# Scores of two neighbouring attention maps, issued together in different rows of the TensorE array

## The reference, cut to what matters

```python
h = rmsnorm(x, ln1_g[layer])
qa, ka, va, cq, ckv, kr, qc, kc, vc = split(h @ w_in[layer])
out_a = mixer_dilated(...)   # A: 6 heads of width 64, local bands (128,1) (512,4) (2048,16)
out_b = mixer_mla(...)       # B: 6 heads, q and k of width 64 + 32 = 96
out_c = mixer_diff(...)      # C: 4 heads with 2 softmax maps each, q and k of width 32
x = x + concat([out_a, out_b, out_c]) @ w_o[layer]
u = rmsnorm(x, ln2_g[layer]) @ w_up[layer]
x = x + square(relu(u)) @ w_down[layer]
```

## Time and profile before

| | |
|---|---|
| median of 3 runs | 1770.53 us (1770.4 to 1772.18) |
| the profiled execution | 1770.33 us, its span 1768.6 us |
| granted TensorE clock, mean | 0.999 |
| PE busy | 1757.6 us, 99% |
| PEld (weight loads) busy | 1535.5 us, 87% |
| DVE busy | 1157.6 us, 65% |
| ACT busy | 931.6 us, 53% |
| POOL busy | 26.5 us, 1% |
| DMA | 303 MB, mean 171 GB/s |

### The profile page before, as it was taken

How to read it: one execution, slowest core, us unless ns; L and a number is a source line. 1 busy time by engine, 2 the same in 40 slices (tenths; PEclk the granted TensorE clock), 3 DMA queues, 4 the chain that set the end, 5 groups by cost and what they waited for, 6 DMA issues and landing times.

```text
span 1768.6 us, 26182 instructions
## 1 busy us (share of the span) xinstructions
PE 1757.6 (99%) x9886; PEld 1535.5 (87%) x9886; DVE 1157.6 (65%) x1700; ACT 931.6 (53%) x1376; POOL 26.5 (1%) x32
## 2 busy tenths in 40 slices
PE   9999999999999999999999999999999999999998
PEld 8888898898888988898889888889898888989886
DVE  6665588766655666468776664668574746857473
ACT  6554456645544555455655553567553536745352
POOL 0000000000000000000000000000000000000000
PEclk9999999999999999999999999999999999999999
DMA  8755533544555554543345545544355543435551
GB/s 315 214 190 179 203 117 122 190 175 182 186 180 189 191 190 179 202 167 120 134 176 175 190 178 190 185 133 146 116 193 198 184 163 118 145 115 194 197 185 48
DMA packets 45842, 303.04 MB, mean 171 GB/s; under 512 B 5104, under 2 KB 6256, under 8 KB 12312
## 3 DMA queue, kind: packets, MB, share of 16 engines
q1 hardware_dynamic: 45720, 301.36, 48.5%
HBM read 300.02 MB, written 1.31 MB: 170 GB/s over the span
## 4 chain that ended last, share of the span: by engine, by line
PE 97%; DVE 1%; ACT 1%; issue 1%; POOLq 0%; POOL 0%; ACTq 0%; DVEq 0%
PE psG L493 13%; PE psG L495 13%; PE psG L494 13%; PE psG L571 9%; PE psP L571 5%; PE psSO L571 5%; PE psG L577 5%; PE psG L544 3%; PE psG L545 3%; PE psG L546 3%; PE psSO L577 3%; PE psP L577 3%; PE psSO L688 2%; PE psP L610 1%; PE psP L870 1%; PE psSO L894 1%
## 5 line engine op out<-in xcount | busy, mean ns | idle before, releaser
L1596 DVE TENSOR_TENSOR wlo<-raw,whi 128x1024 fp32r<-128x1024 f32 (+4 forms) x388 | 656.6, 1705 | 311.0 <-ACT whi L1074 310.7
L1074 ACT ACTIVATE whi<-raw 128x1024 fp32r<-128x1024 f32 (+4 forms) x388 | 554.0, 1443 | 276.0 <-PE psG L495 162.2
L493 PE MATMUL psG<-whi,x 128*128 128x512 f32 (+3 forms) x544 | 210.8, 387 | 0.0
L495 PE MATMUL psG<-whi,x 128*128 128x512 f32 (+3 forms) x544 | 200.8, 369 | 0.0
L494 PE MATMUL psG<-wlo,x 128*128 128x512 f32 (+3 forms) x544 | 200.4, 368 | 0.0
L493 PE MATMUL psG<-whi,hid_hi 128*128 128x512 f32 x472 | 184.1, 390 | 0.0
L495 PE MATMUL psG<-whi,hid_lo 128*128 128x512 f32 x472 | 183.6, 389 | 0.0
L494 PE MATMUL psG<-wlo,hid_hi 128*128 128x512 f32 x472 | 183.6, 389 | 0.0
L571 PE MATMUL psG<-x,whi 128*128 128x512 f32 x704 | 179.8, 392 | 0.0
L544 PE MATMUL psG<-x,wlo 128*128 128x256 f32 x512 | 147.5, 288 | 1.5 <-DVE wlo L1596 1.5
L571 PEld LDWEIGHTS psG<-x,whi 128*128 128x128 f32 x704 | 126.6, 189 | 22.6
(11 more groups left out here) (380 smaller groups left out, 2778.7 us busy)
## 6 DMA issues: line engine op xcount, KB each, us to landing
raw<-in_w SPq DMA_DIRECT2D x261, 1024.0 KB, 4.8
raw<-in_w SPq DMA_DIRECT2D x12, 768.0 KB, 4.2
raw<-in_w SPq DMA_DIRECT2D x14, 512.0 KB, 3.3
raw<-in_w SPq DMA_DIRECT2D x4, 576.0 KB, 3.8
raw<-in_w SPq DMA_DIRECT2D x4, 432.0 KB, 3.2
bias<-line_scratch SPq DMA_DIRECT2D x8, 192.0 KB, 10.1
h<-in_x SPq DMA_DIRECT2D x2, 512.0 KB, 5.6
out<-h SPq DMA_DIRECT2D x2, 512.0 KB, 2.7
```

The source lines that it names most:

```text
L493: e.matmul(o, ph, wh, start=first, stop=False)
L495: i = e.matmul(o, pl, wh, start=False, stop=last)
L1074: e.activation(w_at(whi, j, off, n), raw[:, j % RAW, off:off + n], ACT.Copy).then_inc(s_hi, count)
L1596: e.tensor_tensor(w_at(wlo, j, off, n), raw[:, j % RAW, off:off + n], f32(w_at(whi, j, off, n)), ALU.subtract).then_inc(s_lo, count)
```

## The change

Maps whose scores use 32 or 64 rows (C and A: n below 8 or from 14) are issued in pairs. At the even map's step PE takes two banks, for n and n + 1, and issues the matmuls in the order: first query block of n, first of n + 1, second of n, second of n + 1. The odd map's step issues no scores. The order of everything else on PE within a step stays. B stays as it was. On DVE each map's scores are still read in that map's own step, but the wait is for the scores of the pair's second map in both cases.

```diff
+def paired(n):
+
+    return n < 8 or n >= 14
@@ tensor
             def scores2(l, n):
-                q, kk, _, _, _ = map2(n)
+
+                if paired(n) and n % 2:
+                    return
                 e.wait_ge(s_prep, prep_value(l, "qc", 0) if n < 8 else prep_value(l, "qb", 2) if n < 14 else prep_value(l, "ka", 1))
-                b = spare(("s2", l, n))
+                ns = (n, n + 1) if paired(n) else (n,)
+                bs = [spare(("s2", l, m)) for m in ns]
                 for t, c0, w in SEGS:
-                    i = e.matmul(TB[b][:, c0:c0 + w], q[:, t * 128:t * 128 + 128], kk[:, 0:w], start=True, stop=True)
-                i.then_inc(s_tp, 1)
-                spare_frees(b, (s_mx, 2 * (16 + 20 * l + n) + 2))
+                    for m, b in zip(ns, bs):
+                        q, kk, _, _, _ = map2(m)
+                        i = e.matmul(TB[b][:, c0:c0 + w], q[:, t * 128:t * 128 + 128], kk[:, 0:w], start=True, stop=True)
+                        if t == 1:
+                            i.then_inc(s_tp, 1)
+                for m, b in zip(ns, bs):
+                    spare_frees(b, (s_mx, 2 * (16 + 20 * l + m) + 2))
@@ vector
             def scores2(l, n):
                 m = 16 + 20 * l + n
                 bs = map2(n)[2]
-                u, b = TBU["s2", l, n]
+                b = TBU["s2", l, n][1]
+
+                u = TBU["s2", l, n | 1 if paired(n) else n][0]
```

## The result

The changed kernel takes 1759.24 us (1759.03 to 1759.66, 4 runs) against 1770.51 us of the kernel before (1770.4 to 1772.18): ratio 0.9935, 95% interval 0.9922 to 0.9947, 11.3 us less. The forecast was 1762.4 us: the right way and within its range (1758.8 to 1766.8), but 3.2 us too little. The sum behind it had two wrong terms, one in each direction.

The account below looks back on a forecast made before the run. PE's own order of work was taken as the bound. Fewer visits 5.6 us plus overlap 3.1 us less new waits 0.6 us gave 8.1 us off the median of 1770.53: 1762.4 us, range 1758.8 to 1766.8.

Parts of the forecast that it names:

- The bound: The order of work on PE sets the end; PE is busy for 1757.6 of 1768.6 us.
- Step 1: PE, scores of C and A: 28 visits to part of the rows become 14, saving 0.40 us each, 5.6 us.
- the rival of 0.2 us for each: Inside a pair on PE, each change of rows costs as much as a mode change: 1773.9 us; chance 0.07.
- Step 2: PE, inside a pair: the two maps' records overlap only at borders, 0 to 0.44 us; 0.22 taken, 3.1 us in all.
- Step 3: PE taking two banks at once causes no new waits: 0 us, upper end 0.3 us.
- Step 4: DVE reads an even map's scores about 0.4 us later, relative to their start; covered by 1.9 us of room.
- Step 5: ACT and DVE must keep up with an earlier PE, tightest at values of map 5: 0.6 us of new waits allowed.
- Step 6: Weight pieces, DMA and the blocks behind move forward with PE's own progress: 0 us.
- The first rival: Inside pairs on PE, full overlap at all three borders: 11.8 less some 0.9 us of waits, 1759.6 us; chance 0.22.

Follow-up runs that it names:

- experiment 8: Changed kernel, but scores of B taken over the first 64 of their 96 elements, same columns and number of matmuls: 1763.46 us.
- Experiment 2: Changed kernel, but in each pair both blocks of n are issued before both blocks of n + 1: 1759.81 us.
- Experiment 1: Changed kernel, but the odd map of each pair uses the even one's q and k, so both use the same rows: 1766.24 us.
- Experiment 3: Changed kernel, but only the maps of A are paired, those of C issued singly as before: 1765.63 us.
- experiment 5: Changed kernel, but ACT takes c_hi (high part of transposed output columns 3 and 4) before the exponential of map 16: 1758.16 us.

## Why the prediction was right and wrong, point by point

**The bound.** PE's own sequence sets the end: right. 13.0 us less busy gave 11.3 us. The distances of starts and the sums from them hold. One reading of the earlier trace rows was short: the 30 waits of PEld before scores are those of the 28 maps of C and A and the two of map 12 (experiment 8). After the change they are 16, that is 14 and the same two.

**Step 1, fewer visits.** Right, to a few hundredths: 1.70 us for a pair one after the other (forecast 1.68), 1.04 us for a B map in 64 rows (by the sum 0.64 + 0.40). An inner change of rows costs nothing that shows; the rival of 0.2 us for each is out, with 1.05 us for a pair against its 2.3.

**Step 2, overlap inside the pair.** This step failed: "Each float32 matmul is two records that run one after the other in the same rows ... and issue is in order. So b1 can at best run beside a2, a3 beside b2, and b3 beside a4", with at most 0.44 us a pair, of which I took 0.22. In its place a1 runs beside b1, a2 beside b2, and so on, all four: 0.64 us a pair, 0.20 beyond the upper bound that I had given. The two records of a float32 matmul don't behave like two entries of one queue. Experiment 2 shows that a second matmul for the same rows doesn't hold back the other map's first; a queue for each row group would do this, but no run looks at the queues themselves. The choice between the bounds failed as well: from the distance of loads I read one load path; the loads of two row groups start together. That distance was measured among loads for the same rows and said nothing about different ones.

**Step 3, banks.** No wait of PE at L880 on a bank: right.

**Step 4, DVE's read.** No wait of PE at the transposes (L891) on ACT: right.

**Step 5, the others must keep up.** The place, map 5, was named; the price, 0.6 us in all, was 2.5 us, and the second place was missed. For map 5 I took DVE's queue to move with map 5's scores and ACT's q, which would have made it 2.6 us earlier for a PE that is 2.5 us earlier. In the changed kernel its rotations of q are 3.45 us earlier (1191.89 to 1188.44), but the copy of map 4's transposed probabilities behind them waits for PE's transposes of map 4 (1190.57, [0.31 <-PE psP L891]), and these have only the gain of three pairs: the copy is 3.06 us earlier than before (1193.63 to 1190.57), where PE, with the gain of four, would have come to the values of map 5 3.7 us earlier. Experiment 1 shows the rest: the same chain of 4.86 us makes no wait when the pair costs 0.65 us more. So the lead that counts is local. The even step keeps its length and the odd step loses 1.04 us, and a chain that ends behind the odd step shows by as much as this is more than the room it had. Experiment 3 shows this for c_lo, which waits although PE gained nothing before A, and experiment 5 removes it.

**Step 6, pieces.** PE waits for no low part of a weight piece (L1608) in the second mixers: right. The c_lo of the second new wait is the low part of the other operand.

**The sum.** 14 x (0.40 + 0.22) - 0.6 = 8.1 was forecast; what stands in its place is 14 x 0.97 - 2.5 = 11.1 us, with the growth seen at 12 pairs as the gain of one. The two errors had opposite signs: 14 x 0.35 = 4.9 us too little gained, 1.9 too little lost. The first rival's 1759.6 us came within 0.4 us of the measured time with the same two errors, so its time is no proof of it.

The half rule of the Trainium skill that no row could show before (TensorEngine Tiling, Key Properties: a change of tile within a mode does not drain) agrees with the trace after, 0.01 us between records of different rows. So does what the Trainium skill says in TensorE: Matmul & The Clock Gate, The mechanism, on starts some 4 ns apart in different row groups, with 0.00 to 0.01 us here. I had read it as a rule about borders only. The statement in the same section of the Trainium skill that matmuls keep the order of the program in start and end does not hold for the starts in experiment 2 (ends are modelled in these traces and decide nothing): all of map 16 (psSO) was issued ahead of map 17 (psP), yet 17's second record starts at 1239.77, before 16's third at 1239.87.

## What to carry to other kernels

In this kernel float32 score matmuls with a contraction of 64 or less cost a visit of 0.40 us into part of the array and back; with the neighbour's scores in other rows and another bank beside them, the second map was free. It paid even for operands padded with zeros to full rows, where a pair took 1.26 us instead of 1.72. When work is moved from one step of a hand-written order into another, look for what was covered by it in the step that it leaves: a wait comes there, by what was moved (here 1.04 us) less the room that the chain had (0.3 to 0.7 us were lost each time), although DVE and ACT are busy for 66% and 53% of the span. Find for each such chain where on PE it begins: that start moves with PE too.

## What the runs showed of the hardware that I had not expected

Two float32 score blocks in different rows run record by record beside each other, loads included, 1.05 us for two instead of 1.04 for one. They do so even when both blocks of one map are issued before the first of the other (1759.81 against 1759.24 us). Map 8's scores over 64 rows cost 0.40 us more than the same over 96, but map 12's, behind transposes, only 0.16 us more.
